# Who makes the low halves of the first feed-forward weights, and the order of evictions in the last unit

## The reference

```python
    h2 = rmsnorm(x, norm_ffn[l])
    gate, up = jnp.split(h2 @ w_ffn_in[l], 2, axis=-1)       # 1024 -> 2 x 2816
    x = x + (jax.nn.silu(gate) * up) @ w_ffn_out[l]
return rmsnorm(x, norm_final)
...
    mod = jax.nn.silu(c) @ w_ada[l] + b_ada[l]               # second block
    x = x + gate[:, None] * (y @ w_out[l])
return rmsnorm_2(x, final_g)
```

## Time and profile before

| | |
|---|---|
| median of 3 runs | 1350.56 us (1350.37 to 1352.68) |
| the profiled execution's own time | 1350.47 us |
| its span | 1348.7 us |
| granted TensorE clock | 0.999 of full speed |
| PE busy | 1331.6 us (99%), 8182 matmuls |
| DVE / ACT / POOL busy | 744.9 / 573.8 / 442.2 us |
| L460, POOL's low parts | 97 instructions, mean 4404 ns |
| L1511, DVE's first addition of an ada tile | 24 instructions, 104.6 us, mean 4357 ns |
| L1225, DVE's low parts | 12 instructions |

### The profile page before, as it was taken

The page is one execution under the profiler, slowest core; times in us unless marked ns, Lnnn a source line. Parts: engine busy times, 40 slices in busy tenths (PEclk is TensorE's granted clock), DMA queues, the critical chain, the costliest instruction groups (busy, mean ns, idle before and its releaser), DMA issues.

```text
span 1348.7 us, 21206 instructions
## 1 busy us (share of the span) xinstructions
PE 1331.6 (99%) x8182; PEld 1096.6 (81%) x8182; DVE 744.9 (55%) x1243; ACT 573.8 (43%) x786; POOL 442.2 (33%) x118
## 2 busy tenths in 40 slices
PE   8999999999999999999999999999999999999997
PEld 6888989888888888888888877777888888888885
DVE  4643242664466888888844472335677777102445
ACT  5644353361243222222323255556555655433233
POOL 5421222234443444444444413322211111444441
PEclk9999999999999999999999999999999999999999
DMA  6231312214235555554433342232232222223221
GB/s 194 88 93 63 93 62 93 93 49 167 86 91 156 140 140 140 140 140 130 117 91 102 105 109 78 83 104 63 64 86 69 62 80 76 65 93 120 99 94 63
DMA packets 201671, 134.31 MB, mean 100 GB/s; under 512 B 5720, under 2 KB 195017, under 8 KB 201623
## 3 DMA queue, kind: packets, MB, share of 16 engines
q1 hardware_dynamic: 200390, 131.41, 33.4%
q10 hardware_dynamic: 848, 1.60, 0.4%
q0 software_dynamic: 384, 0.64, 0.2%
HBM read 131.51 MB, written 2.12 MB: 99 GB/s over the span
## 4 chain that ended last, share of the span: by engine, by line
PE 89%; issue 6%; DVE 2%; POOL 2%; ACT 0%; DMA 0%; POOLq 0%; DVEq 0%; ACTq 0%
PE acc L482 19%; PE acc L483 19%; PE acc L484 19%; PE acc L491 4%; PE acc L493 3%; PE acc L492 3%; POOL wlo L460 2%; PE acc L506 1%; PE acc L505 1%; PE acc L507 1%; PE acc L1905 1%; PE acc L1906 1%; PE acc L1907 1%; PE acc L2444 1%; PE acc L2446 1%
## 5 line engine op out<-in xcount | busy, mean ns | idle before, releaser
L460 POOL TENSOR_TENSOR wlo<-raw,whi 128x2048 fp32r<-128x2048 f32 (+1 forms) x97 | 427.2, 4404 | 864.9 <-ACT whi L456 864.8
L482 PE MATMUL acc<-hhi,whi 128*128 128x512 f32 x928 | 370.4, 399 | 1.9 <-issue 1.9
L484 PE MATMUL acc<-hhi,wlo 128*128 128x512 f32 x928 | 361.6, 390 | 0.0
L483 PE MATMUL acc<-hlo,whi 128*128 128x512 f32 x928 | 361.6, 390 | 0.0
L456 ACT ACTIVATE whi<-raw 128x2048 fp32r<-128x2048 f32 (+1 forms) x110 | 203.6, 1851 | 111.4 <-PE acc L484 92.0
L482 PEld LDWEIGHTS acc<-hhi,whi 128*128 128x128 f32 x928 | 174.3, 188 | 41.2 <-issue 6.5
L483 PEld LDWEIGHTS acc<-hlo,whi 128*128 128x128 f32 x928 | 174.4, 188 | 37.8 <-issue 3.1
L484 PEld LDWEIGHTS acc<-hhi,wlo 128*128 128x128 f32 x928 | 174.2, 188 | 36.7
L1511 DVE TENSOR_TENSOR ada<-ada 128x512 f32<-128x512 f32 x24 | 104.6, 4357 | 0.8
L491 PE MATMUL acc<-hhi,whi 128*128 128x512 f32 x224 | 92.7, 414 | 0.8 <-DVE wlo L1225 0.8
L493 PE MATMUL acc<-hhi,wlo 128*128 128x512 f32 x224 | 87.8, 392 | 0.0
(11 more groups left out here) (388 smaller groups left out, 2153.3 us busy)
## 6 DMA issues: line engine op xcount, KB each, us to landing
raw<-in_w_in_dram SPq DMA_DIRECT2D x56, 512.0 KB
raw<-in_w_in_dram SPq DMA_DIRECT2D x26, 1024.0 KB
raw<-in_w_ffn_in_dram SPq DMA_DIRECT2D x44, 512.0 KB
ada<-in_w_ada_dram SPq DMA_DIRECT2D x24, 512.0 KB, 3.8
raw<-in_w_ffn_out_dram SPq DMA_DIRECT2D x16, 704.0 KB
raw<-in_w_out_dram SPq DMA_DIRECT2D x8, 1024.0 KB
xnat<-in_x_dram SPq DMA_DIRECT2D x8, 512.0 KB, 6.3
raw<-in_w_branch_gla_dram SPq DMA_DIRECT2D x4, 1024.0 KB
```

The costliest lines, as they stand in the source:

```text
L460: nc.gpsimd.tensor_tensor(wlo[:, slot, 0:n], raw[:, slot, 0:n], whi[:, slot, 0:n].bitcast(f32), ALU.subtract).then_inc(s_unit_lo, 1)
L482: nc.tensor.matmul(acc[bank][:, :], h, xh[:, k, :], start=(k == 0), stop=False)
L483: nc.tensor.matmul(acc[bank][:, :], h, xl[:, k, :], start=False, stop=False)
L484: last = nc.tensor.matmul(acc[bank][:, :], lo, xh[:, k, :], start=False, stop=(k == nk - 1))
```

## The change

GpSimd stops after unit 34 in the feed-forward-in stage and starts again with unit 56. VectorE makes the low parts of units 35 to 55, each behind `alo` of the unit before; the last two, which belong to the second feed-forward product, have 1408 columns. For this VectorE's loop has its first and last pass written out. In the last unit group ScalarE squares rows 0 and 1 of the first half ahead of the last split, and VectorE evicts all four banks before the first of the products with the gain.

```diff
@@ ScalarE, last unit group
             split_hi(act, U_OUT2 + 2, 0, lin=first_tile(U_OUT2))
-            split_hi(act, U_OUT2 + 3, 1, lin=first_tile(U_OUT2) + TT)
...
             for t in range(TT):
+                if t == 2:
+                    split_hi(act, U_OUT2 + 3, 1, lin=first_tile(U_OUT2) + TT)
                 z_square(0, t)
@@ VectorE
-            def dve_low(u, slot):
+            def dve_low(u, slot, n=16 * P):
...
-            with dve.Fori(0, FT // 2) as i:
+            def gate_up(i, lows, n=16 * P):
                 for j in range(2):
...
+                    if j in lows:
+                        dve_low(i * 2 + (U_FIN + 2 + j), j, n)
+
+            gate_up(0, (1,))
+            with dve.Fori(1, FT // 2 - 1) as i:
+                gate_up(i, (0, 1))
+            gate_up(FT // 2 - 1, (0, 1), FT // 2 * P)
...
             for t in range(TT):
                 z_tile(0, t)
-                if t > 0:
-                    y_first(t - 1)
-            y_first(TT - 1)
+            for t in range(TT):
+                y_first(t)
@@ GpSimd
-            unit_pairs(U_BR, U_FOUT)
-            unit_pairs(U_FOUT, U_ATT, FT // 2 * P)
+            unit_pairs(U_BR, U_FIN + 2)
+            split_lo(pool, U_FIN + 2, 0)
+            pool.wait_ge(s_unit_lo, U_FOUT + 2)
+            unit_pairs(U_FOUT + 2, U_ATT, FT // 2 * P)
```

More of the change, by code:

```diff
@@ L1218, in hold @@
                 V.memset(tick[:, a * 6:a * 6 + 1], 0.0)
-            def dve_low(u, slot):
+            def dve_low(u, slot, n=16 * P):
                 dve.wait_ge(s_unit_lo, u)
                 dve.wait_ge(s_unit_hi, u + 1)
-                V.tensor_tensor(wlo[:, slot, :], raw[:, slot, :], whi[:, slot, :].bitcast(f32), ALU.subtract)\
+                V.tensor_tensor(wlo[:, slot, 0:n], raw[:, slot, 0:n], whi[:, slot, 0:n].bitcast(f32), ALU.subtract)\
                     .then_inc(s_unit_lo, 1)
```

## The result

Time after, five runs: median 1343.94 us (1343.41 to 1344.40), where 1343.9 was forecast. The kernel before took 1350.56 us (1350.04 to 1352.68) beside it, so the ratio is 0.9947, 95% interval 0.9932 to 0.9961. The profiled execution took 1343.41 us with a span of 1341.6, 7.06 us less than before (1350.47).

A forecast was written before the change was run, and what follows sets the result against it. With PE 99% busy, it took a VectorE, ScalarE and GpSimd ring to pace the feed-forward-in stage, plus a last-group wait. Terms 3.9 + 2.7 = 6.6 us; 1350.47 - 6.6 = 1343.9 us, range 1343.0 to 1347.3 (forecast's own 1343.2 to 1344.9).

The forecast's parts named there:

- The nine waits put down to nothing: Feed-forward-in loop returns: TensorE's sequencer, held for VectorE's late ada sum, shows 0.37 us at each of nine returns.
- Rival A: Feed-forward-in loop: returns keep their cost, 3.3 us stay, gain only 3.3, 1347.2 us; chance 0.10.
- A ring through VectorE: Feed-forward-in stage: VectorE, ScalarE and GpSimd pace it at 11.28 us a unit; TensorE alone would take 11.13.
- Rival B: Feed-forward-in stage keeps its pace altogether; only the last unit's 2.7 us is gained, 1347.8 us; chance 0.05.
- term 1: Feed-forward-in stage: twenty units at TensorE's 11.13 us instead of 226.5 us in all, 3.9 us gained.
- The ring's size: Feed-forward-in stage after the change: 10.37 us a unit, say 10.5 with 0.1 to 0.2 for register instructions and a semaphore.
- The slack: VectorE's ring in the feed-forward-in stage has 0.6 us of slack, hiding the 21 low parts, 48 us of work.
- The cover of the ada sum: Feed-forward-in loop: sum ends 8.3 us (8.5 with additions) behind L1531, wanted at 11.13; cover 2 us.
- The low part on VectorE at 2.28 us: Feed-forward-in stage: each of 21 low parts takes VectorE 2.28 us, the last two shorter; 48 us of work, hidden.
- Rival D: Feed-forward-in stage: VectorE's subtraction takes longer than 2.28 us; at 4.60 us the kernel is slower, 1377 us; chance 0.04.
- Term 2: Last unit group: TensorE's wait for its third bank's eviction goes whole, 2.7 us gained.
- Rival C: Last unit group: the wait only moves, as the split waits for a square; 1346.6 us; chance 0.04.

The follow-up runs named there:

- slack_3: Kernel after with three PSUM fills on VectorE (1.57 us together) behind each low part of the loop's 18 units: 1357.82 us, ratio 1.0049.
- ada_lag: Kernel before, but TensorE takes the ada sum in the middle of the next gate tile instead of ahead of the loop return: 1351.37 us, ratio 0.9996.
- ada_first: Kernel before with the next unit's ada tile ahead of VectorE's wait for `ahi`; GpSimd still makes every low part: 1348.42 us, ratio 0.9975.
- slack_1: Kernel after with one PSUM fill on VectorE (0.48 us) behind each low part of the loop's 18 units: 1344.04 us, ratio 0.9947.
- low_again: low_only run once more, unchanged, for its spread: 1347.19 us, ratio 0.9970, in two groups of four runs.
- tail_only: Kernel before with only the last unit group's new order: 1347.67 us, ratio 0.9976.
- low_only: Kernel after with the last unit group in its old order: 1348.34 us, ratio 0.9976.

## Why the prediction was right, step by step

- **The nine waits put down to nothing are the tail of a late sum.** Shown. With the sum early they are gone (0.14 us behind the small matmul instead of 0.51); with the sum made late again (slack_3) nine waits of 1.9 us in total are back. The 0.14 us is also what stands at the stage's end, where no return is the earlier trace rows, so the return itself adds nothing that shows. In the whole stage before, a unit that begins with a return takes 11.5 us and the one after it 11.13. Rival A falls. The Trainium skill (page "Runtime: NRT & Kernel Launch", section "Instruction fetch mechanics") speaks of a stall where the target of a taken branch is not in the pages that the engine holds; no such stall shows in this loop, and no run tells where its target lay.
- **A ring through VectorE paces the stage.** Shown twice: a later place for the sum bought only a part (ada_lag), and a shorter ring without moving the low parts bought all of it (ada_first). Rival B falls with the stage's 11.136 us a unit. The ring before was 11.32 us in the mean; the 11.28 of the prediction is the shorter of two units that alternate, which changes nothing in its sum, since term 1 was taken from TensorE's rows.
- **The ring's size.** 10.21 us against 10.37, and 10.5 with the additions. The steps were right within 0.1 us (2.21 to the ada tile for 2.28, 2.64 for 2.65, 3.29 for 3.33); the 0.1 to 0.2 us added for register instructions was not needed. The slack, 0.92 us against 0.6 forecast, lies between the two fills of slack_1 and slack_3. The cover of the ada sum was 2.6 us against 2.
- **The low part on VectorE at 2.28 us.** 2.29 us in 19 of 21 instructions and 1.62 in the short ones. Rival D falls. slack_3, with its ring at 11.93 us, shows its mechanism at work: 13.7 us in the stage.
- **Term 1, 3.9 us.** 3.79 by the trace; 1350.1 - 1346.4 = 3.7 by the runs of low_again without the fall, and 1352.2 - 1348.2 = 4.0 by those of ada_first, which has it. The tenth that is missing by the trace is 20 units at 11.136 for 11.13 us.
- **Term 2, 2.7 us.** 2.73 by the trace, and 1350.1 - 1347.67 = 2.4 by the times of tail_only. Rival C falls with the trace after the change: the split keeps its place and no wait of TensorE is left in the group. But the step was right for one kind of execution of the kernel before only. Its standstill of 2.4 us is followed, in some executions, by half the clock for some 3.4 us; by their times, and by the trace of ada_lag, these are the 40 of 64. The profiled execution and the first median stood in the other group. Against the runs with the fall the change gains 1352.2 - 1344.0 = 8.2 us, against those without it 6.1. The prediction had no such term, and that it was worked out on an execution without the fall was luck.
- **The sum.** 6.6 us forecast, 7.06 between the two profiled executions, of which 0.34 lie at the start and 0.20 between stage and last group, where nothing was changed. By the times of like runs the gain is 6.1 us, 0.5 less than forecast, and the base of 1350.47 us was 0.4 above the mean of its own group: the two errors nearly cancel. That 1343.9 met a median of 1343.94 is luck to that extent; the two terms are not. In the prediction's chances, those named for "faster" add up to 0.905 and not to 0.89, which moves nothing else.
- **Who makes the low parts was not what mattered.** The prediction gave the low parts to VectorE as a cost that is hidden and took the gain from the ada tile running with GpSimd idle. ada_first shows that the tile's place alone would have done. Likewise only one of the last group's two edits was needed.

## What to carry to other kernels

On an engine that is 99% busy, look for a stretch where the feeding engine never waits for it: that engine may set the pace there, even if the only trace of it is a few waits put down to nothing at loop returns. Before moving work to another engine, see which instruction is slow only because of its neighbour in time (here 5.01 us for 0.69) and try to move that one. Where a kernel has a short standstill of TensorE, time it often and read the clock of each run: one profiled execution can be of the rarer kind.

## What the runs showed of the hardware

- A TensorE standstill of 2.4 us was followed in some executions and not in others by a granted clock of half (1.2 for 2.4 GHz) over 3.4 us. Four traces have it (low_only, low_again, ada_lag, ada_first) and one with the same standstill has not (before). It began at TensorE's new start in low_only and 1.4 us after it in ada_lag. By the groups of times, 40 of 64 runs of the kernel before had it, 10 of 11 of low_only, 4 of 8 of low_again, 9 of 11 of ada_lag and 11 of 11 of ada_first; with the standstill filled, none of 11; without it, none of the 10 of tail_only and the 10 of the kernel after. Price: 1.5 to 1.6 us by the traces, about 2.0 by the times. What decides it from one run to the next is not known.
- VectorE and GpSimd held each other up both ways here, where VectorE's instruction had both inputs in SBUF, and whoever started second paid most: a VectorE sum of 0.69 us took 5.01 beside a GpSimd subtraction of 4.60 and ended 0.5 us after it; eight subtractions of 4.90 us in all took 8.93; and GpSimd's 4.6 became 5.03 to 5.09 where VectorE had started first. The Trainium skill, page "SBUF — State Buffer", section "Who interferes with whom", says that a VectorE instruction with two SBUF inputs contends with a GpSimd instruction that reads SBUF, and that the order of issue decides who is blocked; the numbers agree with it.
- The same subtraction of 128x2048 f32 values takes 2.29 us on VectorE and 4.60 on GpSimd.
